# Value projections with the activations stationary: an experiment on a fused transformer kernel

## The reference

```python
# block 1: HGRN2, 16 heads of 128
u = rmsnorm(x, w) @ w_in;  q, f_fwd, f_bwd, v, g = split(u)
o = chunked_gated_recurrence(q, 1 - f, log f, v)       # both directions, summed
# short MLP with a depthwise convolution over tokens
# block 2: stick-breaking attention (8 heads of 128) beside a gated delta rule
sq, sk, sv, gq, gk, gv, gz, gb, ga = split(rmsnorm_2(x, mix_norm) @ w_in_2)
weights = exp(log_beta + later);  out = einsum('bhqs,bshd->bqhd', weights, sv)
# cross attention over 256 memory tokens, 4 heads of 128
q = rmsnorm_2(x) @ w_q;  k, v = split(rmsnorm_2(mem) @ w_kv)
p = softmax(q k^T / sqrt(128));  o = einsum('bhsm,bmhd->bshd', p, v);  x += o @ w_o
# second MLP with a convolution, final norm
```

## Time and profile before

| | |
|---|---|
| median of 3 runs | 2946.23 us (2945.1 to 2947.05) |
| the profiled execution's own time | 2941.11 us |
| its span, first to last instruction | 2939.3 us |
| PE busy | 2848.2 us, 97% of the span |
| PEld / DVE / ACT / POOL busy | 84% / 68% / 50% / 2% |
| mean granted TensorE clock | 0.988 |
| DMA | 479.50 MB, mean 163 GB/s |

### The profile page before, as it was taken

The page is one execution under the profiler, slowest core; times in us unless marked ns, Lnnn a source line. Parts: engine busy times, 40 slices in busy tenths (PEclk is TensorE's granted clock), DMA queues, the critical chain, the costliest instruction groups (busy, mean ns, idle before and its releaser), DMA issues.

```text
span 2939.3 us, 46768 instructions
## 1 busy us (share of the span) xinstructions
PE 2848.2 (97%) x16372; PEld 2473.9 (84%) x16372; DVE 1995.8 (68%) x2756; ACT 1480.8 (50%) x1698; POOL 64.7 (2%) x89
## 2 busy tenths in 40 slices
PE   7999999998999999999989999999999999999997
PEld 6888888886888888888878888887888888888886
DVE  4777677766888888744445676768578888886443
ACT  4444444446555555434345545566465555554443
POOL 0000000000000000000000000000000000000000
PEclk9999999999999999999989999999999999999999
DMA  6444444442555555555525543344545555555553
GB/s 203 158 151 151 139 150 143 150 146 85 191 182 198 180 191 193 194 185 181 184 74 170 164 138 120 117 144 149 165 141 181 191 180 190 181 192 194 183 180 117
DMA packets 130163, 479.50 MB, mean 163 GB/s; under 512 B 14480, under 2 KB 14496, under 8 KB 129648
## 3 DMA queue, kind: packets, MB, share of 16 engines
q1 hardware_dynamic: 129600, 473.14, 49.0%
q0 software_dynamic: 432, 4.53, 0.4%
HBM read 475.51 MB, written 2.10 MB: 162 GB/s over the span
## 4 chain that ended last, share of the span: by engine, by line
PE 85%; DVE 5%; ACT 5%; issue 3%; POOL 1%; DMA 0%; DVEq 0%; SPq 0%; ACTq 0%
PE acc L354 50%; PE acc L356 26%; ACT whi L294 2%; PE ps L761 2%; PE ps L421 1%; DVE KQ L674 1%; POOL KM L1643 1%; DVE KQ L675 1%; DVE wlo L300 1%; PE ps L1250 1%; PE ps L1243 1%; DVE m L504 0%; ACT hs L381 0%; DMA raw<-stream 0%; DVE x L508 0%
## 5 line engine op out<-in xcount | busy, mean ns | idle before, releaser
L354 PE MATMUL acc<-hs,whi 128*128 128x512 f32 x5056 | 1806.2, 400 | 8.8 <-DVE hin L327 4.5
L300 DVE TENSOR_TENSOR wlo<-raw,whi 128x1024 fp32r<-128x1024 f32 x896 | 1072.0, 1222 | 655.5 <-ACT whi L294 647.5
L356 PE MATMUL acc<-hs,wlo 128*128 128x256 f32 x5056 | 1424.6, 282 | 0.0
L294 ACT ACTIVATE whi<-raw 128x1024 fp32r<-128x1024 f32 x896 | 931.9, 1055 | 835.8 <-PE acc L356 824.5
L354 PEld LDWEIGHTS acc<-hs,whi 128*128 128x128 f32 x5056 | 954.6, 189 | 232.6 <-issue 10.0
L356 PEld LDWEIGHTS acc<-hs,wlo 128*128 128x128 f32 x5056 | 958.0, 189 | 0.8 <-issue 0.7
L354 PE MATMUL acc<-acts,whi 128*128 128x512 f32 x1408 | 499.6, 398 | 0.0
L356 PE MATMUL acc<-acts,wlo 128*128 128x256 f32 x1408 | 396.2, 281 | 0.0
L354 PEld LDWEIGHTS acc<-acts,whi 128*128 128x128 f32 x1408 | 264.3, 188 | 65.2
L308 ACT ACTIVATE half<-acc 128x512 f32<-128x512 f32 x218 | 130.2, 597 | 350.0 <-PE acc L356 348.2
L356 PEld LDWEIGHTS acc<-acts,wlo 128*128 128x128 f32 x1408 | 265.4, 189 | 0.3
(11 more groups left out here) (278 smaller groups left out, 2038.7 us busy)
## 6 DMA issues: line engine op xcount, KB each, us to landing
raw<-stream SPq DMA_DIRECT2D x896, 512.0 KB, 3.4
x<-xT SPq DMA_DIRECT2D x1, 2048.0 KB, 8.0
memr<-memT POOLq DMA_DIRECT2D x1, 2048.0 KB, 10.1
outT<-sq POOLq DMA_DIRECT2D x1, 2048.0 KB, 6.5
vec<-vecs SPq DMA_DIRECT2D x1, 489.0 KB, 8.3
KQ<-masks SPq DMA_DIRECT2D x1, 448.0 KB, 9.9
cst<-consts SPq DMA_DIRECT2D x1, 256.0 KB, 8.9
neg<-consts POOLq DMA_DIRECT2D x1, 192.0 KB, 2.7
```

The source lines that it names most:

```text
L294: nc.scalar.activation(whi[:, b, :], raw[:, b, :], ACT.Copy).then_inc(hi_ready, 1)
L300: nc.vector.tensor_tensor(wlo[:, b, :], raw[:, b, :], whi[:, b, :].bitcast(F32), ALU.subtract).then_inc(lo_ready, 1)
L354: nc.tensor.matmul(acc[:, 2 * par + n, :], whi[:, b, c:c + P], src[:, kt, :], start=(kt == 4 * first), stop=False)
L356: mm = nc.tensor.matmul(acc[:, 2 * par + n, 0:T], wlo[:, b, c:c + P], src[:, kt, 0:T], start=False, stop=(kt == 4 * last + 3))
```

## The change

The weight groups of the values are multiplied the other way round. `weigh_tokens` makes 128 tokens of the high activations stationary and streams the 256 high and the 256 low weight columns as one operand of 512 columns, in two runs; then 128 tokens of the low activations are stationary and 256 high weight columns stream. The result has tokens as partitions. Transposes and copies go, and with them the waits for them. The inverse norm is now needed as a column for each token: for HGRN2 two matmuls with one column and a copy to `rrn` make it in the first stage (`factor_tensor`, `factor_vector`), the mixed block has one already (`rrc`), and the memory is normalised beforehand. `whi` and `wlo` become two parts of one tensor.

```diff
-        whi = sb("whi", [P, SLOTS, BLK], F32R)
-        wlo = sb("wlo", [P, SLOTS, BLK], F32R)
+        wts = sb("wts", [P, 2, SLOTS, BLK], F32R)
+        whi, wlo = wts[:, 0], wts[:, 1]
...
+        def by_token(ap):
+            return ap.rearrange("p c (h d) -> p c h d", h=2)
...
+        def evacuate_tokens(dve, dest, group, par, plain, scale):
+            sum_halves(dve, group, par, plain)
+            nc.vector.tensor_tensor(dest, by_token(half[:, par]),
+                                    scale.unsqueeze(2).unsqueeze(3).broadcast_to([P, 2, 2, P]),
+                                    ALU.mult).then_inc(evac, 1)
...
+        def weigh_tokens(c, b, q, src, kt, par, start, stop):
+            w = slice(q * 256, (q + 1) * 256)
+            nc.tensor.matmul(acc[:, 2 * par + c, :].rearrange("p (s n) -> p s n", s=2),
+                             src[:, kt, c * P:(c + 1) * P], wts[:, :, b, w], start=start, stop=False)
+            return nc.tensor.matmul(acc[:, 2 * par + c, 0:T], src[:, kt, T + c * P:T + (c + 1) * P],
+                                    whi[:, b, w], start=False, stop=stop)
...
         def hg_scalar(act, turn, par):
-            yield from pause(2)
-            act.wait_ge(hg_pe.sem, hg_pe.count("vt", turn))
-            nc.scalar.activation(vn[:].rearrange("p a b -> p (a b)"), ps[:, 1, :], ACT.Copy).then_inc(hg_act.sem, 1)
-            yield from pause(2)
+            yield from pause(4)
...
         def hg_tensor(pe, turn, par):
             n = hin[:, par]
-            yield from pause(3)
+            yield from pause(6)
             pe.wait_ge(hg_vec.sem, hg_vec.before(turn))
-            pe.wait_ge(evac, GROUP_AT["hg"] + 5 * turn + 4 + 3)
-            for a in range(4):
-                mm = nc.tensor.transpose(ps[:, 1, a * P:(a + 1) * P], n[:, 4, a * P:(a + 1) * P], ident)
-            mm.then_inc(hg_pe.sem, 1)
-            yield from pause(3)
-            pe.wait_ge(hg_act.sem, hg_act.count("vn", turn))
             pe.wait_ge(hg_vec.sem, hg_vec.count("ks", turn))
...
+        def factor_tensor(pe):
+            yield from pause(10)
+            pe.wait_ge(norm_act.sem, norm_act.count("n1_r"))
+            for c in range(2):
+                mm = nc.tensor.matmul(ps[:, 1, c:c + 1], rr[:, c * P:(c + 1) * P], ident[:, 0:1],
+                                      start=True, stop=True)
+            mm.then_inc(hg_rr, 1)
+        def factor_vector(dve):
+            yield from pause(8)
+            dve.wait_ge(hg_rr, 1)
+            nc.vector.tensor_copy(rrn[:], ps[:, 1, 0:2]).then_inc(hg_rr, 1)
...
         def hg_tensor_out(pe, turn, par):
             pe.wait_ge(hg_act.sem, hg_act.count("ao", turn))
+            pe.wait_ge(evac, GROUP_AT["hg"] + 5 * turn + 4 + 3)
+            vn = hin[:, par, 4].rearrange("p (a d) -> p a d", a=4)
...
         def sb_tensor(pe, t, par):
-            for a in range(4):
-                mm = nc.tensor.transpose(ps[:, 2, a * P:(a + 1) * P], v[:, a * P:(a + 1) * P], ident)
...
         def sb_scalar(act, t, par):
             yield
-            act.wait_ge(sb_pe.sem, sb_pe.count("z", t))
-            nc.scalar.activation(svn[:].rearrange("p a b -> p (a b)"), ps[:, 2, :], ACT.Copy).then_inc(sb_act.sem, 1)
...
         def cross_tensor(pe):
-            def values(p):
+            def outputs(p):
                 pe.wait_ge(evac, GROUP_AT["xv"] + p + 3)
                 pe.wait_ge(xa_act.sem, xa_act.count(f"t{p}"))
-                for h in range(2):
-                    for c in range(2):
-                        mm = nc.tensor.transpose(...)
-            def outputs(p):
-                pe.wait_ge(xa_act.sem, xa_act.count(f"vn{p}"))
...
-            yield
-            values(0)
-            yield from pause(2)
+            yield from pause(3)
             outputs(0)
             yield from pause(5)
-            values(1)
-            yield
             outputs(1)
```

More of the change, by code:

```diff
@@ L334, in evacuate_onto, with multiply @@
             nc.vector.tensor_tensor(dest, dest, half[:, par], ALU.add).then_inc(evac, 1)
-        def multiply(pe, lap, k, group, par, src, kb, first, last, side=None, norm=None):
+        def by_token(ap):
[11 more added lines that the diff above has]
+                                    whi[:, b, w], start=False, stop=stop)
+        def multiply(pe, lap, k, group, par, src, kb, first, last, side=None, norm=None,
+                     tokens=False):
             r, b = at(lap, k)
@@ L352, in multiply @@
                 for q in range(4):
-                    c, kt = q * 256 + n * P, 4 * kb + q
+                    kt = 4 * kb + q
+                    start, stop = kt == 4 * first, kt == 4 * last + 3
+                    if tokens:
+                        mm = weigh_tokens(n, b, q, src, kt, par, start, stop)
+                        continue
+                    c = q * 256 + n * P
                     nc.tensor.matmul(acc[:, 2 * par + n, :], whi[:, b, c:c + P], src[:, kt, :],
-                                     start=(kt == 4 * first), stop=False)
+                                     start=start, stop=False)
                     mm = nc.tensor.matmul(acc[:, 2 * par + n, 0:T], wlo[:, b, c:c + P],
-                                          src[:, kt, 0:T], start=False, stop=(kt == 4 * last + 3))
+                                          src[:, kt, 0:T], start=False, stop=stop)
                 if n == 1:
@@ L553, in body @@
                     else:
-                        multiply(eng, lap, k, g + grp, grp % 2, src, kb, 0, kbs - 1, side, norm)
+                        multiply(eng, lap, k, g + grp, grp % 2, src, kb, 0, kbs - 1, side, norm, name == "xv")
                     if then and kb == kbs - 1:
@@ L819, in hg_all @@
             n = 2 if what == "pe" else 1
-            hg_stage(eng, what, 0, 0, slots(20 * n, take_in(eng, 0, 0)), norm=True)
+            factor = {"pe": factor_tensor, "dve": factor_vector, "act": lambda e: pause(0)}[what]
+            hg_stage(eng, what, 0, 0, slots(20 * n, factor(eng), take_in(eng, 0, 0)), norm=True)
             hg_stage(eng, what, 1, 1, slots(20 * n, attend(eng, 0, 0), take_in(eng, 1, 1)))
@@ L929, in mix_stage @@
                     if kb == 3:
-                        evacuate_scaled(eng, dest(grp), g, par, 16, "n5")
+                        if first < 12 and grp == 2:
+                            eng.wait_ge(gt_vec.sem, gt_vec.count("rr"))
+                            evacuate_tokens(eng, svn[:].rearrange("p (h c) d -> p c h d", h=2), g, par, 16, rrc[:])
+                        else:
+                            evacuate_scaled(eng, dest(grp), g, par, 16, "n5")
                 else:
                     multiply(eng, lap, k_, g, par, hs, kb, 0, 3, side,
-                             "n5" if first == 0 and grp == 0 else None)
+                             "n5" if first == 0 and grp == 0 else None, first < 12 and grp == 2)
             drain(side)
@@ L943, in sb_tensor @@
                 pe.wait_ge(sb_vec.sem, sb_vec.count("lo", t - 1))
-            q, k, v = (sin[:, par, s] for s in range(3))
+            q, k = (sin[:, par, s] for s in range(2))
             for h in range(2):
@@ L947, in sb_tensor @@
                                  start=True, stop=True)
[L948 removed]
+                mm = nc.tensor.matmul(ps[:, h, T:T + P], k[:, h * T + P:(h + 1) * T],
                                  q[:, h * T + P:(h + 1) * T], start=True, stop=True)
[L950 to L951 removed]
             mm.then_inc(sb_pe.sem, 1)
@@ L1369, in weights @@
                                      ps[:, 2 * p:2 * p + 2, :], ACT.Copy).then_inc(xa_act.sem, 1)
-            def values(p):
-                act.wait_ge(xa_pe.sem, xa_pe.count(f"vt{p}"))
-                nc.scalar.activation(xvn[:, 2 * p:2 * p + 2].rearrange("p h c n -> p (h c n)"), ps[:, 2 * p, :],
-                                     ACT.Copy).then_inc(xa_act.sem, 1)
             def outputs(p):
@@ L1606, in _ @@
             side = cross_vector(dve)
-            product(dve, "dve", "xv", 4, 1, 2, dest=kv[:, 4:8], side=side)
+            product(dve, "dve", "xv", 4, 1, 2, dest=xvn, side=side)
             drain(side)
```

37 lines of the change are left out of this document (23 added, 14 removed).

## The result

The changed kernel takes 2926.12 us (median of 5, 2922.1 to 2928.93) against 2945.1 us for the kernel before beside it: a ratio of 0.9934, 95% interval 0.9922 to 0.9947, 19 us faster. The prediction was 2937.0 with a range from 2931: the direction was right, and the gain twice what was forecast and outside the range.

What follows compares the result with a forecast made beforehand. The prediction took PE, busy 97% of the span, to pace the kernel; -6.2 (transposes) - 2.1 (wait) - 1.4 (cross attention) + 0.5 (added matmuls) = -9.2 us, giving a median of 2937.0 us, range 2931 to 2946.

Steps and rivals of the forecast that it cites:

- What stays: HGRN2 loop's back edges: DVE's 3.6 us, PE's hole and the half-clock stretch behind it remain, as the loop is the same.
- rival 4: All 56 transposes: each is worth its record, 15.2 us instead of 6.2; -18.2, 2928.0 us; chance 0.03.
- Transposes: HGRN2, stick-breaking and cross attention: 14 sets of four removed at 0.44 us each, 6.2 us saved, lower bound 5.0.
- The wait for the copied values: HGRN2, seven turns: PE's wait at line 752 for ACT's copy to `vn` goes, 0.30 us each, 2.1 us saved.
- HGRN2 passes the gain on: HGRN2's level steps: their waits move forward with PE, so its 3.5 + 2.1 us gain is taken in full.
- rival 2: HGRN2 keeps its time because level-step waits grow by what goes ahead of them: -3.6, 2942.6 us; chance 0.15.
- End of the cross attention: `outputs(1)` now precedes `heads(1, 0)`, which fits into PE's idle hole: 1.4 us saved, bounds 0 and 1.4.
- Factor matmuls: Added once in HGRN2's first stage: two one-column matmuls issued as four instructions cost 0.5 us, upper bound 0.86.
- The new pairs: 448 pairs in the new form: two-run moving operand costs nothing; either rhythm possible, plus or minus 2.7 us, taken as zero.
- Rival 5: New-form pairs: the moving operand's second run restarts at 0.08 us each, +36 us, 2973 us; chance 0.05.
- The difference between profiled execution and median: Whole kernel: the median shown, 2946.23, lies 5.1 us above the profiled execution's 2941.11; carried over unchanged.
- Rival 3: A long stretch changes rhythm: first up projection turning slow costs 8.3 us, 2945.3 (chance 0.12); second turning quick, 2928.7 (0.05).

Runs made afterwards that it cites:

- experiment 2: The changed kernel with 24 instructions that do nothing ahead of PE's first matmul, loop untouched: 2932.70 us, ratio 0.9949 to the kernel before.
- experiment 4: The kernel before, without the change, with 230 do-nothing instructions ahead of PE's first matmul and 40 ahead of DVE's first work: 2945.88 us, ratio 1.0000.
- experiment 1: The kernel before, unedited, timed and traced a second time: 2946.38 us, ratio 1.0002.
- experiment 11: The changed kernel with four transposes put back ahead of HGRN2's diagonal matmuls, nobody waiting for them: 2935.3 us, ratio 0.9969 to the kernel before.
- experiment 5: The kernel before with the change in stick-breaking and cross attention alone, HGRN2 as before: 2939.19 us, ratio 0.9982.
- experiment 7: The changed kernel with the second up projection's 1408 pairs also in the new form, computing something else: 2921.1 us, ratio 0.9921 to the kernel before.
- experiment 3: The changed kernel with 4 instructions that do nothing ahead of DVE's first work: 2929.55 us, ratio 0.9941 to the kernel before.

## Why the prediction was wrong

**The step that failed** is "What stays": "DVE's 3.6 us at the two back edges of the HGRN2 loop, PE's hole there and the stretch at about half the granted clock behind it: the loop is the same." The loop was not the same. It was 17 PE instructions shorter, and the hole was PE fetching its program again. I had read the row as a property of the loop and never asked what made it. It is worth 8.0 to 8.2 us where the clock falls behind both holes (experiments 2 and 4, and the first trace), 6.2 to 6.4 where behind one (experiments 1 and 11), 4.6 where behind none (experiment 5): half to four fifths of the missing 10, of which the new pairs are another 1.5. No rival held it; rival 4's 2928.0 came near the result by another cause, which experiment 11 refutes.

**Transposes**, 0.44 a set: right in kind, a little small. Experiment 11 has 0.5 a set in HGRN2; stick-breaking lost 0.43 to 0.61 a step, of which 0.41 stands in the half block with the set (3.05 to 2.64 us in the first step) and the rest is the pairs' rhythm. The Trainium skill's 275 ns for a transpose (TensorE: Matmul & The Clock Gate, section Part 4: PE-mode transpose) would be 1.1 a set, an estimate from the page: experiment 11 has less than half.

**The wait for the copied values**, 0.30 a turn: right; 0.84 us left each of stages 2 and 7, against 0.74 forecast for transposes and wait together.

**HGRN2 passes the gain on**: right; rival 2 fell in every turn.

**End of the cross attention**: 1.85 forecast for the order and one set of transposes, 1.87 measured in xo, and 0.55 in xv, some 0.43 for the other set and the rest for the pairs' rhythm.

**Factor matmuls**, +0.5: right. The first stage grew by 0.2 only, but the half block with the four and the next grew by 0.44 (from 1.41 each to 1.77 and 1.49 us), and the stage's value group, in the new form, gave 0.21 back. The upper bound, 0.86, was read from line 904's records, 0.6 us from first to last; the kernel before had half the clock there, and at full clock the four lie 0.3 us from first to last.

```profile
1522.00:1526.20 4.20, 4.20 (x22) 4.20 (x21) 0.00 (x0) 0.00 (x0) 0.00 (x0) 0.50 0.37 125
```

**Evacuations**, zero: the broadcast along the innermost axis took 693 ns, as the plain one did.

**The new pairs**, zero with 2.7 either way: mis-sized. They are always quick: 0.21 us less in the first stage's value group, some 0.05 in each later one of HGRN2, where the normal pairs had taken both rhythms, 0.12 to 0.21 in stick-breaking's, about -1.5 in all (experiment 4 against after). Experiment 7 holds the full price, 8.4 us for 1408 pairs, which would be 2.7 for these. **Rival 5** fell with it.

**The difference between profiled execution and median**, 5.1 us carried over unchanged: most of it was rhythm. The profiled execution had its first up projection in the quick rhythm (490.83); every later trace with the pairs in this order has 498.7 to 499.1. Against experiment 1's profiled execution, 5.0 us longer, that is 8.2, less 3.4 for two half-clock stretches more in the first, one in HGRN2's loop and one in the mixed block. Rival 3's event happened between the profiled executions of before and after and cost 8.2 us, where it was priced at 8.3; with after's profiled execution the slowest of its five, that is why their difference, 12.2 us, is smaller than that of the medians, 19. The change did not cause it, since experiment 1 has it without the change.

The ledger for the median, each from clean stages: HGRN2 outside the jumps -0.57 - 7 x 0.85 + 0.2 = -6.3, stick-breaking -1.7, cross attention -2.4, jumps back -4.6 to -8.2: -15.0 to -18.6, against 19 measured with an interval of 15.6 to 23. So some 10 of the 19 us are the change's own work, as forecast; that the shortened loop also stopped being fetched again was luck, which nothing in the forecast foresaw. Within that also lie the stretches at half clock behind other waits of PE (3.4 us each, some 1.7 us of time), which come and go between executions of one kernel.

## What to carry to other kernels

A stall at a loop's jump with no releaser is worth a look at the instruction queues before it is called constant: whether instruction packets move during the loop is one line of the DMA view, and if they do, shortening the body or moving it by some instructions may be worth more than any single edit in it. Read a second execution of the kernel before ahead of trusting one stretch's pace, and don't trust a releaser that ended just ahead of a restart until a second trace shows it again. Where groups wait in a stream of matmuls, the order of the matmuls ahead of them is a free knob: here it gave some 24 us more, again as much as the change.

## What the runs showed of the hardware

- A loop of PE's program of 1730 instructions was not fetched again; with 24 more ahead of it, it was, in every iteration, 15 packets in 270 us, with 2.3 to 2.6 us between two starts on PE at the jump, and in 6 of 10 cases 3.4 us at 0.5 of the clock behind it: 4.6 to 8.2 us for two jumps. That seven blocks stay and eight do not rests on the fitted offset; that 24 instructions make the difference does not.
- DVE's loop fetched again puts 3.1 and 3.3 us between two of its starts at the jumps (0.6 without) and costs the kernel nothing while PE has work (experiment 3).
- Pairs of 512 and 256 columns with weights stationary have two rhythms at full clock, 347 and 353 ns, one and the same program; with activations stationary they had 347 in all 56 blocks and over a stage of 1408 pairs. In fours of one size a trace showed 350.6 in both up projections, in eights 351.4.
